# A two-block float32 model on one core: order of the attention units, of the first input, of a mixer's weights and of the last gate unit

## The reference

```python
def diff_attention(q, k, v, rel_bias, lam):          # 8 heads, two maps each, d = 64
    # blocks of 128 queries; keys up to the end of the query's 64-chunk are allowed
    logits = einsum(q, k) * d ** -0.5 + bias
    logits = where(allowed, logits, NEG_INF)
    p = softmax(logits)
    attn = p[:, :, 0] - lam * p[:, :, 1]
    return einsum(attn, v)
# k, v = split(rms_norm(h, kv_norm) @ w_kv); q = rms_norm(h, b_norm_pre) @ w_q
# then o = rms_norm(o, subln_w) * (1 - lam_init); mix = o @ w_out
...
h = rmsnorm(x, mix_pre_norm); z = h @ w_in           # cq, ckv, kr, and conv gates b, c, x
q = rmsnorm(z_cq, q_norm) @ w_uq; kv = rmsnorm(z_ckv, kv_norm) @ w_ukv
c = b * conv3(c_gate * xv)
m = concat(rmsnorm(a, attn_group_norm), rmsnorm(c, conv_group_norm)) @ w_out
...
e = rmsnorm(p @ w_ple_proj, ple_norm)
x = x + sigmoid(x @ w_ple_gate) * e                  # the output
```

## Time and profile before

| what | value |
|---|---|
| median of 3 runs | 1073.61 us (1071.01 to 1073.74) |
| profiled execution: its own time | 1073.17 us |
| profiled execution: span, first to last instruction | 1071.4 us |
| TensorE (PE) busy | 1017.5 us, 95% |
| VectorE (DVE) busy | 734.1 us, 69% |
| ScalarE (ACT) busy | 550.2 us, 51% |
| GpSimd (POOL) busy | 91.7 us, 9% |
| mean granted TensorE clock | 0.993 |

### The profile page before, as it was taken

How to read it: one execution, slowest core, us unless ns; L and a number is a source line. 1 busy time by engine, 2 the same in 40 slices (tenths; PEclk the granted TensorE clock), 3 DMA queues, 4 the chain that set the end, 5 groups by cost and what they waited for, 6 DMA issues and landing times.

```text
span 1071.4 us, 18148 instructions
## 1 busy us (share of the span) xinstructions
PE 1017.5 (95%) x6659; PEld 921.8 (86%) x6659; DVE 734.1 (69%) x1097; ACT 550.2 (51%) x822; POOL 91.7 (9%) x95
## 2 busy tenths in 40 slices
PE   6999999999999999777999999998998999999997
PEld 5999988888888998776788888997997788888886
DVE  4687677877745577644787754467857887776466
ACT  4743255655454465443565544344556565556444
POOL 5123101000101100000100010101000100000010
PEclk9999999999999999998999999999999999999999
DMA  8443334556565744322366665624533366665641
GB/s 248 132 137 119 119 118 138 166 188 195 177 196 180 234 148 148 98 80 73 117 214 194 186 189 185 189 67 126 177 99 103 114 192 194 183 195 172 192 148 60
DMA packets 163758, 165.74 MB, mean 155 GB/s; under 512 B 6736, under 2 KB 161504, under 8 KB 163696
## 3 DMA queue, kind: packets, MB, share of 16 engines
q1 hardware_dynamic: 162496, 163.47, 49.8%
q0 software_dynamic: 1056, 1.16, 0.5%
q10 hardware_dynamic: 144, 0.26, 0.1%
HBM read 163.79 MB, written 1.08 MB: 154 GB/s over the span
## 4 chain that ended last, share of the span: by engine, by line
PE 86%; DVE 8%; issue 3%; ACT 3%; DMA 0%; POOL 0%; DVEq 0%; ACTq 0%; POOLq 0%
PE ps L591 30%; PE ps L590 15%; PE ps L574 4%; PE ps L575 4%; PE ps L576 4%; PE ps L587 3%; PE ps L811 3%; PE ps L570 2%; PE ps L569 2%; PE ps L568 2%; DVE w_lo L1790 2%; PE ps L708 2%; PE ps L588 2%; PE ps L581 1%; PE ps L583 1%
## 5 line engine op out<-in xcount | busy, mean ns | idle before, releaser
L1790 DVE TENSOR_TENSOR w_lo<-w_raw,w_hi 128x1024 fp32r<-128x1024 f32 (+3 forms) x318 | 381.0, 1203 | 188.0 <-ACT w_hi L1279 183.0
L1279 ACT ACTIVATE w_hi<-w_raw 128x1024 fp32r<-128x1024 f32 x302 | 317.4, 1054 | 231.4 <-PE ps L591 91.4
L591 PE MATMUL ps<-xs,w_hi 128*128 128x512 f32 x840 | 296.9, 396 | 0.0
L590 PE MATMUL ps<-xs,w_lo 128*128 128x256 f32 x840 | 235.7, 281 | 0.0
L591 PEld LDWEIGHTS ps<-xs,w_hi 128*128 128x128 f32 x840 | 157.8, 188 | 34.5
L591 PE MATMUL ps<-us,w_hi 128*128 128x512 f32 x498 | 175.1, 397 | 0.0
L590 PEld LDWEIGHTS ps<-xs,w_lo 128*128 128x128 f32 x840 | 158.2, 188 | 5.2 <-DVE xs L1923 1.7
L590 PE MATMUL ps<-us,w_lo 128*128 128x256 f32 x498 | 139.2, 280 | 0.0
L574 PE MATMUL ps<-xs,w_hi 128*128 128x256 f32 x384 | 113.5, 296 | 5.7 <-DVE w_lo L1790 4.5
L591 PEld LDWEIGHTS ps<-us,w_hi 128*128 128x128 f32 x498 | 93.5, 188 | 22.3
L575 PE MATMUL ps<-xs,w_hi 128*128 128x256 f32 x384 | 110.1, 287 | 0.0
(11 more groups left out here) (375 smaller groups left out, 1709.4 us busy)
## 6 DMA issues: line engine op xcount, KB each, us to landing
w_raw<-in_mlp_w_up SPq DMA_DIRECT2D x64, 512.0 KB, 4.4
w_raw<-in_mlp_w_down SPq DMA_DIRECT2D x64, 512.0 KB, 3.5
w_raw<-in_a_w_in SPq DMA_DIRECT2D x32, 512.0 KB, 3.9
w_raw<-in_w_gate SPq DMA_DIRECT2D x22, 512.0 KB, 3.7
w_raw<-in_w_up SPq DMA_DIRECT2D x22, 512.0 KB, 4.6
w_raw<-in_w_down SPq DMA_DIRECT2D x20, 512.0 KB, 4.3
w_raw<-in_w_kv SPq DMA_DIRECT2D x16, 512.0 KB, 4.4
w_raw<-in_w_in SPq DMA_DIRECT2D x16, 512.0 KB, 3.9
```

Source lines behind the costliest of these rows:

```text
L590: mm(ps[:, bank, 0:S], lo[:, kk, w], x[:, kt, 0:S], start=False, stop=False)
L591: o = mm(ps[:, bank, :], hi[:, kk, w], x[:, kt, :], start=False, stop=last)
L1279: o = fn(dst, raw, ACT.Copy)
L1790: return v.tensor_tensor(d, x, y, ALU.subtract)
```

## The change

In attention all keys and queries but the values come first in `STREAM`, so that the twelve groups run without a break; values(0) to (2) move to q = 18, 20 and 22, and the banks of pairs 1 and 2 are exchanged. Each slot of ScalarE and VectorE converts quantum q + 3 instead of q + 4. The queries are scaled by minus an eighth (a scaled copy of the norm factor in `rstd2`), so that the logits are negated: the minimum stands for the maximum, the exponential has scale -1 and takes the minimum as its bias, and the instruction that negated the maximum goes; the stored bias has the opposite sign. At the start the identity and the gain row are loaded first, on ScalarE's queue, and `xs` is made from PSUM; the copies to `h` come later, and the table of functions is loaded ahead of the waits. In the second mixer `c0` and `uq` are converted ahead of the norm, after `cq` is taken. In `out2` `take2(5)`, `square_tok(1)` and the order of `take_ple` move. The last unit of `pg` is made by token, in two tiles of 128 tokens; `h` and `ple` of its columns are transposed beforehand, the rest of the rows between its tiles and after it, and the result goes out in five stores. The diff, cut to its core:

```diff
-          ("ak0", 0, 0), ("ak1", 0, 0), ("av0", 0, 0), ("aq0", 0, 0), ("aq1", 0, 0), ("ak2", 0, 0), ("aq2", 0, 0), ("ak3", 0, 0),
-          ("aq3", 0, 0), ("av1", 0, 0), ("av2", 0, 0), ("av3", 0, 0), ("b_out", 1, 4), ("up1", 1, 16), ("down1", 4, 4),
+          ("ak0", 0, 0), ("ak1", 0, 0), ("ak2", 0, 0), ("aq0", 0, 0), ("aq1", 0, 0), ("aq2", 0, 0), ("ak3", 0, 0), ("aq3", 0, 0),
+          ("av0", 0, 0), ("av1", 0, 0), ("av2", 0, 0), ("av3", 0, 0), ("b_out", 1, 4), ("up1", 1, 16), ("down1", 4, 4),
...
-DIFF_SCORE_BANK, DIFF_TURN_BANK, PAIR_BANK = ((2, 3), (6, 7)), 4, (5, 5, 7, 4)
+DIFF_SCORE_BANK, DIFF_TURN_BANK, PAIR_BANK = ((2, 3), (6, 7)), 4, (5, 7, 5, 4)
...
+                    pe.wait_ge(max_ready, N_GROUPS)
+                elif j == 2:
                     pe.wait_ge(xs_ready, XS0["attn"] + 1)
-                elif j > 1:
-                    pe.wait_ge(max_ready, N_GROUPS)
...
-                if 8 <= q <= 16:
+                if 8 <= q < 8 + N_GROUPS:
                     scores(q - 8)
-                elif 18 <= q <= 20:
-                    scores(q - 9)
-                if 11 <= q <= 19:
+                if 11 <= q < 11 + N_GROUPS:
                     turn(q - 11)
-                elif q >= 21:
-                    turn(q - 12)
-                if q in (14, 20, 22):
-                    values((14, 20, 22).index(q))
-                if q in (17, 22):
-                    turn_pair((17, 22).index(q))
-
-            def second_pair():
+                if q in (18, 20, 22):
+                    values(q // 2 - 9)
+                if q in (21, 22):
+                    turn_pair(q - 21)
+
+            def last_pairs():
+                values(3)
                 turn_pair(2)
-                values(3)

             stream("b_out", xs_b, waits=xs_wait("attn"), two=True,
-                   between={1: second_pair, 5: lambda: turn_pair(3)})
+                   between={1: last_pairs, 5: lambda: turn_pair(3)})
...
+            narrow("c0", 1).then_inc(w_used, 1)
             sums("cq")
-            narrow("c0", 1).then_inc(w_used, 1)
...
+            def turn_last():
+                pe.wait_ge(xs_ready, XS0["last"] + KT)
+                for n, (src, bank) in enumerate(((h, B5), (ple, B7))):
+                    for m in range(2):
+                        for t in range(2):
+                            o = nc.tensor.transpose(ps[:, bank, m * S + t * P:m * S + (t + 1) * P],
+                                                    src[:, 6 + t, m * P:(m + 1) * P], ident)
+                    o.then_inc(last_turned, 1)
+
+            def turn_rows():
+                pe.wait_ge(pg_mul, 2)
...
+                        o = nc.tensor.transpose(ps[:, 4 + 2 * m, t * P:(t + 1) * P], h[:, t, m * P:(m + 1) * P], ident)
...
+            stream("pg", xs, waits=xs_wait("last"), two=True, after=turn_last, between_tiles=turn_rows)
+            pe.wait_ge(pg_mul, 3)
+            pe.wait_ge(last_taken, 1)
+            for m in range(2):
+                for t in range(2):
+                    o = nc.tensor.transpose(ps[:, B5, m * S + t * P:m * S + (t + 1) * P], h[:, 4 + t, m * P:(m + 1) * P], ident)
+            o.then_inc(row_turned, 1)
...
+            act.dma_start(table[:, 0:P], a["tables"][:, 0:P]).then_inc(ident_in, 16)
+            act.dma_start(vrow_pre[:, :], a["a_norm_pre"][0].rearrange("(a b) -> a b", b=P)).then_inc(pre_in, 16)
+            act.dma_start(table[:, P:T_LEVEL], a["tables"][:, P:T_LEVEL]).then_inc(tab_in, 16)
...
+            root_tables()
...
-                high_w(xs, V_A_PRE, None, [j])
+                act.wait_ge(x_turned, j + 1)
+                for t in range(2):
+                    o = fn(xs[:, 2 * j + t, 0:S], ps[:, 4 + j, t * S:(t + 1) * S], ACT.Copy,
+                           scale=vec[:, V_A_PRE + 2 * j + t:V_A_PRE + 2 * j + t + 1])
+                o.then_inc(xs_hi, 1)
...
-            hi_d(7)
...
-                hi_d(q + 4)
-                if q == 6:
-                    take_v(0)
-                if q in (20, 22):
+                hi_d(q + 3)
+                if q in (22, 23):
+                    high_pair(q - 22)
+                if q in (18, 20, 22):
                     take_v(q // 2 - 9)
-                if 12 <= q <= 20:
+                if 12 <= q < 12 + N_GROUPS:
                     copy_turned(q - 12)
-                elif q >= 22:
-                    copy_turned(q - 13)
-                if 9 <= q <= 17:
+                if 9 <= q < 9 + N_GROUPS:
                     exps(q - 9)
-                elif 19 <= q <= 21:
-                    exps(q - 10)
-                if q in (15, 21, 23):
-                    square_pair((15, 21, 23).index(q))
-                if q in (16, 22):
-                    root_pair((16, 22).index(q))
-                if q in (18, 23):
-                    high_pair((18, 23).index(q))
+                if q in (19, 21, 23):
+                    square_pair((q - 19) // 2)
+                if q in (20, 21, 23):
+                    root_pair((20, 21, 23).index(q))
+            hi_d(27)
...
+            narrow_high("cq", V_Q, 0)
             hi(UNIT0["c0"], part=0)
-            narrow_high("cq", V_Q, 0)
-            root("mix_pre")
             hi(UNIT0["c0"], part=1)
-            narrow_high("ckv", V_KV2, 2)
             for part in range(2):
                 hi(UNIT0["uq"], part=part)
+            root("mix_pre")
+            narrow_high("ckv", V_KV2, 2)
...
-            square_tok(1)
             high("conv", 0, cy, xs_m)
             high("conv", 1, cy, xs_m)
+            square_tok(1)
+
+            def take_ple(j):
+                fn(ple[:, 2 * j:2 * j + 2, :], ps[:, PLE_BANK[j], :].rearrange("p (a t) -> p a t", a=2), ACT.Copy)\
+                    .then_inc(z_act, 1)
+
+            act.wait_ge(w_used, 2 * (UNIT0["ple"] + 1))
+            take_ple(2)
+            hi(UNIT0["out2"] + 1, part=0)
             act.wait_ge(att_ms, 1)
             link(fn(stat_t[:, 2, :], stat_t[:, 1, :], ACT.Ln))
             fn(stat_t[:, 2, :], stat_t[:, 2, :], ACT.Exp, scale=-0.5).then_inc(att_guess, 1)
-            hi(UNIT0["out2"] + 1, part=0)
-            act.wait_ge(w_used, 2 * (UNIT0["ple"] + 1))
-            for j in range(4):
-                fn(ple[:, 2 * j:2 * j + 2, :], ps[:, PLE_BANK[j], :].rearrange("p (a t) -> p a t", a=2), ACT.Copy)\
-                    .then_inc(z_act, 1)
-                if j == 1:
-                    hi(UNIT0["out2"] + 1, part=1)
+            take_ple(0)
+            take_ple(1)
+            hi(UNIT0["out2"] + 1, part=1)
+            take_ple(3)
...
+            for j in range(3):
+                one("pg", j)
+                act.wait_ge(pg_sum, j + 1)
+                fn(mo[:, 2 * j:2 * j + 2, :], mo[:, 2 * j:2 * j + 2, :], ACT.Sigmoid).then_inc(pg_sig, 1)
+                if j == 0:
+                    act.wait_ge(last_turned, 1)
+                    fn(rowbuf[:, :, 768:D], ps[:, B5, :].rearrange("p (m c) -> p m c", m=2), ACT.Copy).then_inc(last_taken, 1)
+            act.wait_ge(tail_done, len(POSTS) + 1)
+            fn(mo[:, 6, :], ps[:, LAST_BANK, 0:S], ACT.Sigmoid).then_inc(pg_sig, 1)
...
+            act.wait_ge(w_used, 2 * N_UNITS)
+            fn(mo[:, 7, :], ps[:, LAST_BANK + 1, 0:S], ACT.Sigmoid).then_inc(pg_sig, 1)
+            act.wait_ge(row_turned, 3)
+            fn(rowbuf[:, :, 512:768], ps[:, B5, :].rearrange("p (m c) -> p m c", m=2), ACT.Copy).then_inc(row_copied[1], 1)
...
+            for j in range(4):
+                dve.wait_ge(xs_hi, XS0["x"] + j + 1)
+                for t in range(2):
+                    wcol = V_A_PRE + 2 * j + t
+                    o = v.scalar_tensor_tensor(xs[:, 2 * j + t, S:2 * S], ps[:, 4 + j, t * S:(t + 1) * S], vec[:, wcol:wcol + 1],
+                                               xs[:, 2 * j + t, 0:S].bitcast(F32), ALU.mult, ALU.subtract)
+                o.then_inc(xs_ready, 1)
+                lo(j // 2, part=j % 2)
...
-                                                   -3.0e38, ALU.add, ALU.max, d_max[:, m, qt, hd:hd + 1])
-                link(o)
-                v.tensor_scalar(d_neg[:, :, qt, hs], d_max[:, :, qt, hs], -(D // HEADS // 2) ** -0.5, None, ALU.mult)\
-                    .then_inc(max_ready, 1)
+                                                   3.0e38, ALU.add, ALU.min, d_min[:, m, qt, hd:hd + 1])
+                o.then_inc(max_ready, 1)
...
-            lo_d(7)
+            link(v.tensor_scalar(rstd2[:, :], rstd[:, :], -(D // HEADS // 2) ** -0.5, None, ALU.mult))
...
-                if 9 <= q <= 17:
+                if q in (22, 23):
+                    low_pair(q - 22)
+                if 9 <= q < 9 + N_GROUPS:
                     add_bias(q - 9)
-                elif 19 <= q <= 21:
-                    add_bias(q - 10)
                 if q == 4:
                     take_kq("ak0")
                     take_kq("ak1")
                 elif q % 2 == 0 and DIFF_UNITS[q // 2 - 1][1] != "v":
                     take_kq(DIFF_UNITS[q // 2 - 1])
```

(93 more changed lines are left out.)

64 lines of the change are left out of this document (21 added, 43 removed).

## The result

The kernel after takes 1045.78 us in the median of 4 runs (1043.13 to 1046.83), before 1072.31 (4 runs, 1070.67 to 1073.74): a ratio of 0.975, 95% interval [0.972, 0.978]. The prediction said 1048.5, range 1042 to 1058. The profiled execution of after took 1046.83 us with a span of 1045.0, against 1071.4 before: 26.4 us less, where the working had 24.8.

A forecast was written before the change was run, and what follows sets the result against it. TensorE was taken as busy for most of every slice, so only its idle or slow-clock time could be gained. Terms 19.5 + 1.3 + 2.1 + 1.6 + 0.3 = 24.8 us off 1073.2 gave 1048.4, stated as 1048.5; range 1042 to 1058.

The forecast's parts named there:

- Attention: Quantum 11 to the restart in `b_out`: 16.0 us less idle time and 3.5 of slow clock, 19.5 us saved.
- what was to stay: Attention and `b_out`: waits of 1.6 us for pair 3's low part and 2.4 before the next unit remain.
- The bound of 21.5: Attention's upper bound in us, if the slow stretch of 3.5 us right after the restart in `b_out` goes too.
- Start: First weights: TensorE starts at about 11.2 us instead of 12.96; 1.3 us saved, bounds 0.4 and 1.7.
- The two cases that I weighed: Start: fast pitch begins as long after work starts as before, saving 1.6 us, or at 21.6 again, saving 0.8.
- Second mixer: `c0` and `uq` converted ahead of the norm: 2.1 us saved, bounds 0.5 and 4.2.
- VectorE's tally: Second mixer: VectorE's operations from 728.35 to `ukv`'s low part count 24.6 us, ending at 753.2 instead of 755.3.
- `out2`: `take2(5)` moved behind, `ple2` first: TensorE's second restart at 810.6 instead of 812.3; 1.6 us saved, bounds 0.7 and 2.3.
- Last gate unit: Kernel's end: 2.5 us saved after the last matmul, less 1.0, 1.1 and 0.1: 0.3 us, bounds -1.2 and 1.5.
- Half of the stage: Rival, attention: an omitted latency makes each slot wait 0.6 us, 15 slots give back 9 us: 1057.5; chance 10%.
- The clock still falls: Rival, attention: the clock falls as before, since `b_out` keeps waits; 3.5 us more, 1052; chance 14%.
- Slower: Rival, attention: low parts on VectorE come too late in 15 slots, at 2 us each 1078.5; chance 3%.

The follow-up runs named there:

- the second execution of after: The kernel after run once more, unchanged: 1046.24 us, 0.976 of before; its profiled execution has a span of 1040.8 us.
- the mixer's old order: The kernel after with the second mixer's order of before on all three engines: 1047.19 us, 0.976 of before.
- the gap filled: The kernel after with eight unused identity products between the transposes of x and the first weights: 1045.63 us, 0.975 of before.

## Why the prediction was right, step by step

**Attention: right in cause and size.** Predicted 19.5, measured 20.06: 15.9 of idle time (16.0 in the working) and 4.2 of clock (3.5). The transposes' waits went, what was to stay stayed (1.56 and 2.36 us), and the clock came back. The slot of VectorE, said to be 3.5 us, runs from 412.94 to the end of the low part at 416.46: 3.52. The bound of 21.5, if the slow stretch behind the restart goes too, is what the second execution of after shows. What I had not seen is how little the rest of the edit matters: the reordering of units, the late values and the exchanged pairs, a large part of the diff, are worth 0.7 us.

**Start: the earlier first matmul was right, the size of the term fell together by luck.** First matmul at 11.2 as said, the third low part at 15.0 against 15.1; 1.54 us in the profiled pair, 1.3 predicted. But the term is no constant. With the same instructions the sums begin at 22.0 to 24.7. The two cases that I weighed were a rise tied to the work and a rise that stays in place; the runs show neither.
The Trainium skill ("TensorE: Matmul & The Clock Gate", section "What's actually happening") says that the window runs freely, so that the moment varies from run to run. The table agrees that it varies. But the page gives a variation of 500 ns either way, and here the moments lie 9.4 us apart, so the measurement decides, and why the spread is this wide stays open.

**Second mixer: 2.1 predicted, 2.06 measured, with two errors that cancel and luck beside them.** The step that failed is the low part of `uq`, taken as 4.33 us from the earlier trace rows. Those 4.33 us began 0.04 before GpSimd's copy of the rotated key and contained about 1.7 of being held up; in after all seven subtractions there, one for `c0` and six for `uq`, take 3.77. The hold moved with the copy to the Newton step, 1.57 us there, where the same instruction takes 0.43 without it. The sum was the same because I had counted the hold once, in the wrong place. The wait for `c0` was 0.30 instead of 0.6. And the working reads the whole gain as waiting and VectorE's tally, with no term for the clock: 1.25 of the 2.06 us are the slow matmuls behind the wait of 4.2. Had they run at full pace in before, the same reordering would have given some 0.8 us; this is an estimate, 2.06 less 1.25.

**`out2`: right in size**, 1.6 predicted and 1.76 measured; two waits of 0.47 and 0.44 remain, where before had 1.18 and 1.55. No run undoes these moves alone, so this term rests on the traces.

**Last gate unit: 0.3 predicted, 0.6 measured.** The wait before it is 1.00 where I had 1.1, and it is made by the place of two copies: moved, half of it goes. From the last weight matmul to the end 4.0 us pass instead of 6.7, 2.7 less where I had 2.5. No run undoes this part alone.

**The rivals.** Half of the stage: no slot waits. The clock still falls: not inside the stage, 1.00; behind the restart it did in five of eight executions. Slower: VectorE's slot would have had to pass 5.5 us and takes 3.52; a step more in it changes nothing.

## What to carry to other kernels

In these traces an item that had to wait for a slot to come free (ScalarE's conversion, until the end of the quantum) took what stood behind it along: the copy began 0.96 us after that end. So try such an item one step later than its buffer allows (three quanta ahead instead of four) before reordering anything else; here that was 19.4 of 20.0 us, and it cost nothing because its users still found it in time. When a wait is taken away by itself, list what is due next: here 5.6 us of 12 came back that way. When a long wait goes, look also at the pace of the matmuls behind it, which was more than half of the gain in the second mixer. And profile the same kernel twice before a term of one or two us near an idle gap is believed.

## What the runs showed of the hardware that I had not expected

The pitch of the matmuls rose from 0.21 to 0.12 us at any moment between 11.1 and 20.5 us in seven executions with the same instructions. The view of windows doesn't show the slow pitch ahead of the first rise: in after it prints a granted clock of 1.00 from 11 to 20 us, where the pitch is 0.21. Where the pitch falls again after a first rise, it prints it: 0.50 from 15.0 to 18.5 us with the mixer's old order, and 0.50 from 15.8 to 19.2 with the gap filled. So for the start the pitch must be read, not the clock.

After the same wait of 2.36 us the clock was 0.51 to 0.66 in five executions and 1.00 in three; after one of 0.72 us it was 1.00 in the two executions that have it, which are too few to show that the shorter wait is the reason. After the wait of 4.23 us before `uq` it was low in all four executions that have it, 0.50 to 0.62 over the 4.4 to 4.6 us behind it.

And a copy of 64x2048 on GpSimd (2.15 us) held a product of VectorE for 1.57 us; the same copy on ScalarE took 1.91 us and held nothing.
